# Delta rule: gate rows, two block turns and the inverse times the values on four 64x64 quarters of TensorE's array instead of two

## The chip, the cores and the metric

The kernel runs on one core of one Trainium2 chip. The metric is the device time of one execution in microseconds; the time before is the median of three runs.

## The reference

Two networks of two layers each run one after the other on 256 tokens of width 1024, in fp32. Each layer of the first has a feed-forward part, a mixer of three branches, and another feed-forward part. The branch that the change touches is a gated delta rule with 4 heads of width 128, computed in chunks of 64 tokens:

```python
decay = jnp.exp(jnp.where(causal, g_cum[..., :, None] - g_cum[..., None, :], -jnp.inf))
lower = jnp.where(strict, jnp.einsum('nbhid,nbhjd->nbhij', k_beta, k) * decay, 0.0)
rhs = jnp.concatenate([v * beta[..., None], k_beta * jnp.exp(g_cum)[..., None]], axis=-1)
uw = lax.linalg.triangular_solve(eye + lower, rhs, left_side=True, lower=True, unit_diagonal=True)
attn = jnp.einsum('nbhid,nbhjd->nbhij', q, k) * decay
...
v_new = u_c - jnp.einsum('bhcd,bhdv->bhcv', w_c, state)
o_c = jnp.einsum('bhcd,bhdv->bhcv', q_c, state) + jnp.einsum('bhij,bhjv->bhiv', a_c, v_new)
```

256 tokens make 4 chunks, and with 4 heads there are 16 blocks of 64x64. Outside the branch the mixer multiplies gates, `sigmoid(x @ w_gate + b_gate)`, with the branches' projections, and the second network has convolutions, pooling and sparse attention, which the change leaves alone.

## The kernel before, in words

**Weights.** Nearly all the time goes into products with weights that stream from HBM. Each weight tile of 128x1024 fp32 is split by ScalarE (`WH`, L989) and VectorE (`WL`, L1373) into a high and a low part, and TensorE makes three products of it (L467 to L469, L464 to L466, L560 and L561). Up to six split tiles are held, and ScalarE refills one when TensorE has ended with it.

**The delta rule.** `delta` (L3035 on) writes its own steps out by hand and calls `fill(n)` between them. A fill takes a step of the other branches' products with weights (`others`, L2997): gates, products of branch b, then of branch c. Each engine runs its instructions strictly in this written order, so what is queued behind a waiting instruction waits too.

**Blocks.** The 16 blocks lie in tiles of 128x512: chunk c of a pair of chunks on the partitions `HALVES[c]`, eight blocks side by side. The steps in order: sums of the gates (L644 on); `gd_rows` (L658), which spreads them into rows; `gd_decay` on VectorE (L1707), which subtracts the rows from the sums into `gDD` (L1711) and adds the mask (L1715); the products of keys and queries (L685) with their diagonals and square roots; `gd_lower` (L1736), which ends with `gLL` (L1744); `gd_attend` with `gQKD` (L1750); `gd_base` with `gBB` (L1760, L1763); `gd_flip` (L689), which turns the blocks of `gLL` and then of `gQKD` by a product with the identity (L695), and `gd_flipped` on ScalarE (L1131), which copies them to `gLT` and `gAT` (L1134); masks on GpSimd (L2189); five levels of the inverse (`level_first` L706, `level_mid` L1139 and L1141, `level_second` L718, L724, L726, `level_add` L1769 to L1777); `gd_apply` (L729): inverse times values, 128 columns wide (L737), and keys times inverse (L744); `gd_applied` (L1144) copies the results to `gUU` (L1148) and `gWT` (L1152); then the states.

**Quarters.** `HALVES` are the partitions 0 to 63 and 64 to 127. A 64x64 product reads its operands from one half of the partitions and writes PSUM on one half: the quarter of the array. `gd_rows`, `gd_flip` and the first part of `gd_apply` write to the half that they read from, so they use two quarters of the array, in turn. The levels already take all four: `QUADRANTS` (L95) adds the two crossed pairs. Crossed results come out on the other half of the partitions and in a second bank, and are moved back in two instructions of 64 partitions each (`CROSSED`).

**Banks.** PSUM has eight banks, handed out in a queue: `bank` takes the one at the front together with the event that empties it, and `drop` puts it at the end with the event that will.

```python
def bank(self):
    n, emptied = self.banks.pop(0)
def drop(self, b, *events):
    self.banks.append((b.n, list(events)))
```

TensorE waits for a bank's event (`emptied`, L459) before it writes. A branch's product, for instance, is emptied by `MG` (L1850), VectorE's product of gate and branch.

Of the kernel before, what the change touches and what calls it, by code (L numbers as in the profile page):

```python
# [8 lines left out]
ALU = mybir.AluOpType  # L9
# [5 lines left out]
P = 128  # L15
# [82 lines left out]
def csl(g):  # L98
    return slice(g * 64, g * 64 + 64)
# [356 lines left out]
class TensorProgram(Program):  # L456
# [198 lines left out]
            ins = self.e.matmul(k.PS[:, b.n, 16 + 8 * c:24 + 8 * c], chunk, gg, start=True, stop=True)  # L655
        ins.then_inc(*self.s["mm"].up(b.full))

    def gd_rows(self, l, b):  # L658
        k = self.k
        self.wait_ge("gdn_v", (l, "gg"))  # L660
        self.emptied(b)
        for g in range(8):
            for r in HALVES:
                ins = self.e.matmul(k.PS[r, b.n, csl(g)], k.sc["GG"][r, g:g + 1].to_broadcast([64, 64]), k.cm["tri"][r, r],
                                    start=True, stop=True)
        ins.then_inc(*self.s["mm"].up(b.full))

    def gd_turn(self, l, j0, t, b):
        k = self.k
# [16 lines left out]
                                    start=True, stop=True)  # L686
        ins.then_inc(*self.s["mm"].up(b.full))

    def gd_flip(self, l, n, b):  # L689
        k = self.k  # L690
        self.wait_ge("gdn_v", (l, n))
        self.emptied(b)
        for g in range(8):
            for r in HALVES:
                ins = self.e.matmul(k.PS[r, b.n, csl(g)], k.W[n][r, g, :], k.ident[r, r], start=True, stop=True)  # L695
        ins.then_inc(*self.s["mm"].up(b.full))

    def level_first(self, l, n, b, bx):
        k = self.k
# [29 lines left out]
    def gd_apply(self, l, ub, wb):  # L729
        k = self.k  # L730
        self.wait_ge("gdn_v", (l, "bt", 5))
        self.wait_ge("gdn_v", (l, "vbt", 1))
        for t in range(2):
            self.emptied(ub[t])
            for h in range(4):
                for r in HALVES:
                    ins = self.e.matmul(k.PS[r, ub[t].n, tsl(h)], k.W["BT"][r, 4 * t + h, :], k.W["VBT"][r, 4 * t + h, :],  # L737
                                        start=True, stop=True)
            ins.then_inc(*self.s["mm"].up(ub[t].full))
        for b in wb:  # L740
            self.emptied(b)
        for g in range(8):
            for c, r in enumerate(HALVES):
                ins = self.e.matmul(k.PS[:, wb[c].n, csl(g)], k.W["KBE"][r, g, :], k.W["BT"][r, g, :], start=True, stop=True)  # L744
        ins.then_inc(*self.s["mm"].up(wb[0].full, wb[1].full))
# [222 lines left out]
class ScalarProgram(Program):  # L968
# [154 lines left out]
        self.wait_ge("const_v", "eps")  # L1123
        self.e.activation(k.NR, k.NR, ACT.Sqrt, bias=k.eps[1e-6]).then_inc(*self.s["gdn_a"].up((l, "rs")))

    def gd_decay(self, l, b):
        k = self.k
        self.wait_ge("gdn_v", (l, "dm"))
        self.e.activation(k.W["DD"], k.W["DD"], ACT.Exp).then_inc(*self.s["gdn_a"].up((l, "dd")))

    def gd_flipped(self, l, n, to, b):  # L1131
        k = self.k
        self.wait_ge("mm", b.full)
        self.e.activation(k.WF[to], k.PS[:, b.n, :], ACT.Copy).then_inc(*self.s["gdn_a"].up((l, to)))  # L1134

    def level_mid(self, l, n, b, bx):
        k = self.k
# [5 lines left out]

    def gd_applied(self, l, ub, wb):  # L1144
        k = self.k
        for t in range(2):
            self.wait_ge("mm", ub[t].full)
            self.e.activation(k.W["UU"][:, 4 * t:4 * t + 4, :], k.PS[:, ub[t].n, :].rearrange("p (h n) -> p h n", h=4),  # L1148
                              ACT.Copy).then_inc(*self.s["gdn_a"].up((l, "uu", t)))
# [186 lines left out]
class VectorProgram(Program):  # L1336
# [367 lines left out]
        self.wait_ge("gdn_a", (l, "ex"))  # L1704
        self.e.tensor_tensor(tok["B3"], tok["B2"], k.EX[:, 0:8], ALU.mult).then_inc(*up((l, "b3")))

    def gd_decay(self, l, b):  # L1707
        k = self.k
        self.wait_ge("mm", b.full)
        self.wait_ge("gdn_v", (l, "gc"))  # L1710
        self.e.scalar_tensor_tensor(out=k.W["DD"], in0=k.PS[:, b.n, :].rearrange("p (g n) -> p g n", g=8), scalar=-1.0,  # L1711
                                    in1=over(k.sc["GC"], 64), op0=ALU.mult,
                                    op1=ALU.add).then_inc(*self.s["gdn_v"].up((l, "dr")))
        self.wait_ge("gdn_v", (l, "dr"))
        self.e.tensor_tensor(k.W["DD"], k.W["DD"], heads(k.half["decay"], 8),  # L1715
                             ALU.add).then_inc(*self.s["gdn_v"].up((l, "dm")))
# [673 lines left out]
class Walk:  # L2390
# [644 lines left out]
    def delta(self, l, fill, ot, free):  # L3035


        k, e = self.k, self.e
        b = self.bank()
        e.gate_sums(l, b)  # L3040
        e.gate_summed(l, b)
        self.drop(b, ("gdn_v", (l, "gc")), ("gdn_a", (l, "ex")))
        b = self.bank()
        e.gd_rows(l, b)
        e.gd_decay(l, b)
        self.drop(b, ("gdn_v", (l, "dr")))
        b1, b = self.bank(), self.bank()
        e.gd_products(l, 4, 4, b1)
        e.gd_diag(l, 4, "DS", b1)
        e.gd_products(l, 0, 0, b)  # L3050
        e.gd_diag(l, 0, "LL", b)
        self.drop(b, ("gdn_v", (l, "square", 0)))
        fill(2)
        e.gd_factors(l, free)
        b2, bk = self.bank(), [self.bank(), self.bank()]
        e.gd_products(l, 0, 4, b2)
        for t in range(2):
            e.gd_turn(l, 4, t, bk[t])
        fill(2)
        e.gd_lower(l, b1)  # L3060
        self.drop(b1, ("gdn_v", (l, "LL")))
        e.gd_attend(l, b2)
        self.drop(b2, ("gdn_v", (l, "QKD")))
        e.gd_base(l, "bb", "LL")
        fill(3)
        b1, b2 = self.bank(), self.bank()
        e.gd_flip(l, "LL", b1)
        e.gd_flipped(l, "LL", "LT", b1)
        self.drop(b1, ("gdn_a", (l, "LT")))
        e.gd_flip(l, "QKD", b2)  # L3070
        e.gd_flipped(l, "QKD", "AT", b2)
        self.drop(b2, ("gdn_a", (l, "AT")))
        e.gd_keys(l, 0, bk[0])
        self.drop(bk[0], ("gdn_v", (l, "kdc", 0)))
        e.gd_base(l, "bt", "LT")
        fill(2)
        e.gd_keys(l, 1, bk[1])
        self.drop(bk[1], ("gdn_v", (l, "kdc", 1)))
        for t in range(2):
            b = self.bank()  # L3080
            e.gd_turn(l, 8, t, b)
            e.gd_values(l, t, b)
            self.drop(b, ("gdn_v", (l, "vbt", t)))
        fill(2)
        for n, sz in enumerate((2, 4, 8, 16, 32)):
            e.level_mask(l, n, sz)
            b1, b2, last = self.bank(), self.bank(), sz == 32
            e.level_first(l, n, b1, b2)
            fill(2)
            e.level_mid(l, n, b1, b2)  # L3090
            for b in (b1, b2):
                self.drop(b, ("gdn_a", (l, "pw", n)))
            b1, b2 = self.bank(), self.bank()
            e.level_second(l, n, b1, b2, last)
            e.level_add(l, n, b1, b2, last)
            self.drop(b1, ("gdn_v", (l, "bt" if last else "bb", n + 1)))
            self.drop(b2, ("gdn_v", (l, "bt", n + 1)))
            fill(2)
        ub, wb = [self.bank(), self.bank()], [self.bank(), self.bank()]
        e.gd_apply(l, ub, wb)  # L3100
        e.gd_applied(l, ub, wb)
        for n in range(2):
            self.drop(ub[n], ("gdn_a", (l, "uu", n)))
        for n in range(2):
            self.drop(wb[n], ("gdn_a", (l, "wt", n)))
        fill(4)
        for t in range(2):
            bb = self.bank()
            ba = None
            for c in range(2):  # L3110
                if t or c:
                    b = self.bank()
                    ba = ba or self.bank()
                    e.gd_state(l, t, c, b, ba)
                    e.gd_new(l, t, c, b)
                    self.drop(b, ("gdn_v", (l, "vn", 2 * t + c)))
                    fill(2)
                if t and c == 0:
# [445 lines left out]
```

## Time and profile before

| | |
|---|---|
| median of 3 runs | 2267.87 us (2265.51 to 2268.32) |
| profiled execution | 2265.44 us, its span 2263.6 us |
| TensorE busy | 2232.2 us, 99% of the span |
| VectorE busy | 1631.1 us, 72% |
| ScalarE busy | 1198.2 us, 53% |
| GpSimd busy | 129.2 us, 6% |
| mean granted TensorE clock | 0.999 |
| HBM | 179 GB/s over the span |

The profiler's names: PE is TensorE, PEld its weight loads, DVE VectorE, ACT ScalarE, POOL GpSimd. Ends of matmuls are modelled, so starts are what to compare: from the start of one group to the start of the next. A chain of waits goes back from the last instruction, at each step to what released it or to what stood before it on its engine; a piece's length there is how much the end of the run moves past it.

### The profile page before, as it was taken

How to read it: one execution, taken by the hardware profiler on the slowest of the kernel's cores; microseconds unless marked ns; L12 is line 12 of the kernel's file. 1: busy time of each engine (PE TensorE's matmuls, PEld its weight loads, DVE VectorE, ACT ScalarE, POOL GpSimd, SP SyncE). 2: the span in 40 equal slices, each digit the busy share in tenths (PEclk: the TensorE clock that was granted, in tenths of full speed). 3: DMA queues.
4: the chain of work that ended last, by engine and by line, in shares of the span. 5: the costliest groups of instructions: out<-in, count | busy, mean ns of one | idle time of the engine just before them, and what ended most of it. 6: DMA issues, size and time to landing. Idle time of an engine off the chain costs nothing.

```text
span 2263.6 us, 34596 instructions
## 1 busy us (share of the span) xinstructions
PE 2232.2 (99%) x14127; PEld 1910.7 (84%) x14127; DVE 1631.1 (72%) x2503; ACT 1198.2 (53%) x1892; POOL 129.2 (6%) x185
## 2 busy tenths in 40 slices
PE   8999999999999999999999999999999999989999
PEld 7888899877888888888898777888878888867887
DVE  5777767867777776768668867776877778666776
ACT  5555446644555546554356544655454655556553
POOL 2100010120000000000100210000000000420000
PEclk9999999999999999999999999999999999999999
DMA  6755664445565556555564436655655656643654
GB/s 227 224 188 192 197 215 123 142 131 182 190 190 190 185 193 207 186 186 196 194 189 132 141 122 207 201 189 184 211 166 168 205 188 202 195 131 119 197 176 149
DMA packets 283567, 408.17 MB, mean 180 GB/s; under 512 B 13700, under 2 KB 170688, under 8 KB 283152
## 3 DMA queue, kind: packets, MB, share of 16 engines
q1 hardware_dynamic: 275600, 380.91, 52.4%
q0 software_dynamic: 7808, 25.04, 3.6%
q8 instruction: 112, 1.84, 0.3%
q14 instruction: 47, 0.39, 0.1%
HBM read 403.98 MB, written 1.91 MB: 179 GB/s over the span
## 4 chain that ended last, share of the span: by engine, by line
PE 88%; DVE 7%; ACT 3%; issue 1%; DMA 1%; POOL 0%; SPq 0%; DVEq 0%; ACTq 0%
PE PS L561 24%; PE PS L467 12%; PE PS L469 12%; PE PS L468 12%; PE PS L560 11%; PE PS L464 2%; PE PS L466 2%; PE PS L465 2%; DVE WL L1373 2%; PE PS L563 2%; PE PS L484 1%; PE PS L544 1%; PE PS L543 1%; PE PS L542 1%; DVE QX L1670 1%; ACT WH L989 1%
## 5 line engine op out<-in xcount | busy, mean ns | idle before, releaser
L1373 DVE TENSOR_TENSOR WL<-RW,WH 128x1024 fp32r<-128x1024 f32 x682 | 809.9, 1221 | 168.2 <-ACT WH L989 164.0
L561 PE MATMUL PS<-XT,WH 128*128 128x512 f32 x2368 | 807.9, 394 | 0.0
L989 ACT ACTIVATE WH<-RW 128x1024 fp32r<-128x1024 f32 x682 | 685.6, 1042 | 214.9 <-PE PS L469 46.8
L560 PE MATMUL PS<-XT,WL 128*128 128x256 f32 x2072 | 580.8, 280 | 0.0
L561 PEld LDWEIGHTS PS<-XT,WH 128*128 128x128 f32 x2368 | 425.1, 188 | 76.1
L560 PEld LDWEIGHTS PS<-XT,WL 128*128 128x128 f32 x2072 | 389.9, 188 | 13.4
L467 PE MATMUL PS<-WH,XT 128*128 128x512 f32 (+4 forms) x640 | 248.8, 389 | 4.6 <-DVE WL L1373 2.9
L469 PE MATMUL PS<-WH,XT 128*128 128x512 f32 (+4 forms) x640 | 240.0, 375 | 0.0
L468 PE MATMUL PS<-WL,XT 128*128 128x512 f32 (+4 forms) x640 | 239.5, 374 | 0.0
L467 PE MATMUL PS<-WH,HTH 128*128 128x512 f32 x488 | 192.4, 394 | 0.0
L469 PE MATMUL PS<-WH,HTL 128*128 128x512 f32 x488 | 191.7, 393 | 0.0
L468 PE MATMUL PS<-WL,HTH 128*128 128x512 f32 x488 | 191.5, 392 | 0.0
L464 PE MATMUL PS<-XT,WH 128*128 128x256 f32 x560 | 163.2, 291 | 1.6 <-DVE Z L1557 1.0
L1445 DVE TENSOR_TENSOR HM<-PS,HM 128x256 f32<-128x256 f32 x148 | 62.4, 422 | 133.1 <-ACT HM L1026 133.1
L465 PE MATMUL PS<-XT,WL 128*128 128x256 f32 x560 | 157.3, 281 | 0.0
L466 PE MATMUL PS<-XT,WH 128*128 128x256 f32 x560 | 157.2, 281 | 0.0
L467 PEld LDWEIGHTS PS<-WH,XT 128*128 128x128 f32 x640 | 120.8, 189 | 37.6 <-DVE XT L1384 8.9
L1026 ACT ACTIVATE HM<-PS 128x256 f32<-128x256 f32 x148 | 56.7, 383 | 169.8 <-PE PS L561 166.6
L469 PEld LDWEIGHTS PS<-WH,XT 128*128 128x128 f32 x640 | 120.9, 189 | 23.5
L468 PEld LDWEIGHTS PS<-WL,XT 128*128 128x128 f32 x640 | 121.1, 189 | 19.2
L1026 ACT ACTIVATE SG<-PS 128x256 f32<-128x256 f32 x148 | 54.1, 380 | 122.2 <-PE PS L561 120.9
L464 PEld LDWEIGHTS PS<-XT,WH 128*128 128x128 f32 x560 | 106.0, 189 | 6.1 <-issue 2.6
(504 smaller groups left out, 3219.5 us busy)
## 6 DMA issues: line engine op xcount, KB each, us to landing
RW<-in_w_ff_in SPq DMA_DIRECT2D x256, 512.0 KB, 4.4
RW<-in_w_ff_out SPq DMA_DIRECT2D x128, 512.0 KB, 4.5
RW<-in_w_in SPq DMA_DIRECT2D x56, 512.0 KB, 4.7
RW<-in_w_gate SPq DMA_DIRECT2D x48, 512.0 KB, 4.2
RW<-in_ffn_gate SPq DMA_DIRECT2D x44, 512.0 KB, 4.4
RW<-in_ffn_up SPq DMA_DIRECT2D x44, 512.0 KB, 4.3
RW<-in_ffn_down SPq DMA_DIRECT2D x44, 512.0 KB, 4.5
RW<-in_w_out SPq DMA_DIRECT2D x16, 512.0 KB, 4.8
```

The lines of the kernel that those rows point to most:

```text
L464: self.e.matmul(o, wh, xh, start=start, stop=False)
L465: self.e.matmul(o, wl, xh, start=False, stop=False)
L466: return self.e.matmul(o, wh, xl, start=False, stop=stop)
L467: self.e.matmul(o, xh, wh, start=start, stop=False)
L468: self.e.matmul(o, xh, wl, start=False, stop=False)
L469: return self.e.matmul(o, xl, wh, start=False, stop=stop)
L560: self.e.matmul(k.PS[:, b.n, 0:T], wl, k.XTH[:, kt, :], start=False, stop=False)
L561: ins = self.e.matmul(k.PS[:, b.n, :], wh, k.XT[:, kt, :], start=kt == 0, stop=kt == 7)
L989: self.e.activation(u.hi_out, raw, ACT.Copy).then_inc(*self.s["hi"].up(u.n))
L1026: self.e.activation(f[2 + part][:, n, j * T:j * T + T], self.k.PS[:, b.n, 0:T], ACT.Copy).then_inc(*self.s["ffn_a"].up((seq, sl, n, part, j)))
L1373: self.e.tensor_tensor(u.lo_out, raw, u.hi_out.bitcast(F), ALU.subtract).then_inc(*self.s["lo"].up(u.n))
L1445: self.e.tensor_tensor(v, self.k.PS[:, b.n, T:2 * T], v, ALU.add).then_inc(*self.s["ffn_v"].up((seq, sl, n, part, j)))
```

## The change

Three steps of the delta rule take all four quarters. `gd_rows` and both calls of `gd_flip` send half of their blocks (columns 256 to 511) through the crossed quarters into a second bank; `gd_apply` sends the values' second tile (`t = 1`) through the crossed quarters. The number of matmuls is the same. VectorE's subtraction and ScalarE's copies become three instructions each, one of 128x256 and two of 64x256. `gd_applied` copies the second half of `gUU` in two instructions of 64x512, and after `gWT` instead of ahead of it. `gd_rows` and each `gd_flip` take two banks instead of one, so the queue of banks stands otherwise from here on.

```diff
-    def gd_rows(self, l, b):
+    def gd_rows(self, l, b, bx):
...
         self.emptied(b)
-        for g in range(8):
-            for r in HALVES:
-                ins = self.e.matmul(k.PS[r, b.n, csl(g)], k.sc["GG"][r, g:g + 1].to_broadcast([64, 64]), k.cm["tri"][r, r],
-                                    start=True, stop=True)
-        ins.then_inc(*self.s["mm"].up(b.full))
+        self.emptied(bx)
+        for g, (r, to) in product(range(4), QUADRANTS):
+            g, bank = (g, b) if r is to else (g + 4, bx)
+            ins = self.e.matmul(k.PS[to, bank.n, csl(g)], k.sc["GG"][r, g:g + 1].to_broadcast([64, 64]), k.cm["tri"][r, r],
+                                start=True, stop=True)
+        ins.then_inc(*self.s["mm"].up(b.full, bx.full))
...
-    def gd_flip(self, l, n, b):
+    def gd_flip(self, l, n, b, bx):
         k = self.k
         self.wait_ge("gdn_v", (l, n))
         self.emptied(b)
+        self.emptied(bx)
+        for g, (r, to) in product(range(4), QUADRANTS):
+            g, bank = (g, b) if r is to else (g + 4, bx)
+            ins = self.e.matmul(k.PS[to, bank.n, csl(g)], k.W[n][r, g, :], k.ident[r, r], start=True, stop=True)
+        ins.then_inc(*self.s["mm"].up(b.full, bx.full))
...
-        for t in range(2):
-            self.emptied(ub[t])
-            for h in range(4):
-                for r in HALVES:
-                    ins = self.e.matmul(k.PS[r, ub[t].n, tsl(h)], k.W["BT"][r, 4 * t + h, :], k.W["VBT"][r, 4 * t + h, :],
-                                        start=True, stop=True)
-            ins.then_inc(*self.s["mm"].up(ub[t].full))
+        for b in ub:
+            self.emptied(b)
+        for h, (r, to) in product(range(4), QUADRANTS):
+            t = 0 if r is to else 1
+            ins = self.e.matmul(k.PS[to, ub[t].n, tsl(h)], k.W["BT"][r, 4 * t + h, :], k.W["VBT"][r, 4 * t + h, :],
+                                start=True, stop=True)
+        ins.then_inc(*self.s["mm"].up(ub[0].full, ub[1].full))
...
-        self.e.activation(k.WF[to], k.PS[:, b.n, :], ACT.Copy).then_inc(*self.s["gdn_a"].up((l, to)))
+        self.e.activation(k.WF[to][:, 0:256], k.PS[:, b.n, 0:256], ACT.Copy)
+        for r, rx in CROSSED:
+            ins = self.e.activation(k.WF[to][r, 256:512], k.PS[rx, bx.n, 256:512], ACT.Copy)
+        ins.then_inc(*self.s["gdn_a"].up((l, to)))
...
+        self.wait_ge("mm", ub[1].full)
+        for r, to in CROSSED:
+            ins = self.e.activation(k.W["UU"][r, 4:8, :], k.PS[to, ub[1].n, :].rearrange("p (h n) -> p h n", h=4), ACT.Copy)
+        ins.then_inc(*self.s["gdn_a"].up((l, "uu", 1)))
...
+        subtract(slice(0, P), slice(0, P), b, slice(0, 4))
+        for r, to in CROSSED:
+            ins = subtract(r, to, bx, slice(4, 8))
...
-        b1, b2 = self.bank(), self.bank()
-        e.gd_flip(l, "LL", b1)
-        e.gd_flipped(l, "LL", "LT", b1)
-        self.drop(b1, ("gdn_a", (l, "LT")))
-        e.gd_flip(l, "QKD", b2)
-        e.gd_flipped(l, "QKD", "AT", b2)
-        self.drop(b2, ("gdn_a", (l, "AT")))
+        for n, to in (("LL", "LT"), ("QKD", "AT")):
+            b1, b2 = self.bank(), self.bank()
+            e.gd_flip(l, n, b1, b2)
+            e.gd_flipped(l, n, to, b1, b2)
+            for b in (b1, b2):
+                self.drop(b, ("gdn_a", (l, to)))
```

On TensorE at the two turns of layer 0 the instructions and what they wait for stand as follows before. `gLL` and `gQKD` are what is turned, `WH` and `WL` the split weights of the next fill; `s_gdn_v` counts VectorE's steps of the delta rule, `s_gate_v` those on gates and branches, `s_lo` the weights' low parts.

```order
L695 MATMUL PS<-CO,gLL 64x64 [waits s_gdn_v]
L695 MATMUL PS<-CO,gLL 64x64 x15
L695 MATMUL PS<-CO,gQKD 64x64 [waits s_gdn_v]
L695 MATMUL PS<-CO,gQKD 64x64 x15
L467 MATMUL PS<-WH,XT 128x512 [waits s_lo]
```

And in the changed kernel (the function has moved from L695 to L697):

```order
L697 MATMUL PS<-CO,gLL 64x64 [waits s_gdn_v]
L697 MATMUL PS<-CO,gLL 64x64 x15
L697 MATMUL PS<-CO,gQKD 64x64 [waits s_gate_v]
L697 MATMUL PS<-CO,gQKD 64x64 x15
L467 MATMUL PS<-WH,XT 128x512 [waits s_lo]
```

The instructions stand where they stood; the turn of `gQKD` waits for the semaphore of the gates and branches instead of that of the delta rule.

On VectorE, from the subtraction on, before (`GT` are the gates of the two halves of the tokens, `MG` gate times branch, `SX` small tables, `CO` constants):

```order
L1711 SCALAR_TENSOR_TENSOR gDD<-PS,SX 128x512 [waits s_gdn_v,s_mm]
L1715 TENSOR_TENSOR gDD<-gDD,CO 128x512 [waits s_gdn_v]
...
L1744 TENSOR_TENSOR gLL<-PS,gDS 128x512 [waits s_gdn_v]
L1750 TENSOR_TENSOR gQKD<-PS,gDD 128x512 [waits s_mm]
L1760 SCALAR_TENSOR_TENSOR gBB<-gLL,CO 128x512 [waits s_gdn_v]
L1763 TENSOR_TENSOR gBB<-gBB,CO 128x512 [waits s_gdn_v]
L1850 TENSOR_TENSOR MG<-PS,GT_102 128x512 [waits s_gate_a,s_mm]
L1850 TENSOR_TENSOR MG<-PS,GT_103 128x512 [waits s_gate_a,s_mm]
```

And in the changed kernel:

```order
L1721 SCALAR_TENSOR_TENSOR gDD<-PS,SX 128x256 [waits s_gdn_v,s_mm]
L1721 SCALAR_TENSOR_TENSOR gDD<-PS,SX 64x256 x2
L1730 TENSOR_TENSOR gDD<-gDD,CO 128x512 [waits s_gdn_v]
...
L1759 TENSOR_TENSOR gLL<-PS,gDS 128x512 [waits s_gdn_v]
L1765 TENSOR_TENSOR gQKD<-PS,gDD 128x512 [waits s_mm]
L1775 SCALAR_TENSOR_TENSOR gBB<-gLL,CO 128x512 [waits s_gdn_v]
L1778 TENSOR_TENSOR gBB<-gBB,CO 128x512 [waits s_gdn_v]
L1865 TENSOR_TENSOR MG<-PS,GT_102 128x512 [waits s_gate_a,s_mm]
L1865 TENSOR_TENSOR MG<-PS,GT_103 128x512 [waits s_gate_a,s_mm]
```

Only the subtraction differs: three instructions for one. The two `MG` stand fourth and fifth behind `gLL` in both.

## Rows read from the trace of the kernel before

**Rows 1.** The page: busy time, and the chain that ended last by engine.

```profile
PE 2232.2 (99%) x14127; PEld 1910.7 (84%) x14127; DVE 1631.1 (72%) x2503; ACT 1198.2 (53%) x1892; POOL 129.2 (6%) x185
PE 88%; DVE 7%; ACT 3%; issue 1%; DMA 1%; POOL 0%; SPq 0%; DVEq 0%; ACTq 0%
```

**Rows 2.** Chain of waits, layer 0: start us, length us, what.

```profile
417.58 0.70 DVE gDD L1711
...
425.81 2.36 DVE WL L1373 x2
...
428.81 0.70 DVE gLL L1744
429.56 2.08 PE PS L695 x64
431.64 0.43 PE PS L467
...
438.28 0.62 PE PS L706 x32
...
477.50 1.89 PE PS L737 x32
479.39 1.93 PE PS L744 x32
```

**Rows 3.** Timeline of TensorE, layer 0: start, length, operation, idle before.

```profile
414.09 1.15 PE L664 MATMUL PS<-CO,SX 64*64 64x64 f32 x32
415.17 1.55 PE L685 MATMUL PS<-QX 128*64 128x64 f32 x45
...
429.56 1.15 PE L695 MATMUL PS<-CO,gLL 64*64 64x64 f32 x32 [0.31 <-DVE gLL L1744]
```

**Rows 4.** Who waited for whom, TensorE, whole run: total us, times, longest.

```profile
PE PS L724 <- ACT gPW L1141: 1.2, 2, 0.6
```

**Rows 5.** Timeline of VectorE, layer 0: at the subtraction, the turns, the last level.

```profile
418.31 0.78 DVE L1715 TENSOR_TENSOR gDD<-gDD,CO 128x512 f32<-128x512 f32 x1
...
429.42 0.68 DVE L1750 TENSOR_TENSOR gQKD<-PS,gDD 128x512 f32<-128x512 f32 x1
...
431.34 1.28 DVE L1850 TENSOR_TENSOR MG<-PS,GT 128x512 f32<-128x512 f32 x2
...
474.60 0.42 DVE L1774 SCALAR_TENSOR_TENSOR gBT<-PS,gBT 128x256 f32<-128x256 f32 x1 [0.42 <-PE PS L718]
475.93 1.29 DVE L1850 TENSOR_TENSOR GT<-PS,GT 128x512 f32<-128x512 f32 x2
```

**Rows 6.** Timeline of ScalarE, layer 0: a turn's copy, a level's copies, the apply's.

```profile
430.75 0.60 ACT L1134 ACTIVATE gLT<-PS 128x512 f32<-128x512 f32 x1 [1.74 <-PE PS L695]
...
438.98 0.38 ACT L1139 ACTIVATE gPW<-PS 128x256 f32<-128x256 f32 x1 [0.93 <-PE PS L706]
439.37 0.77 ACT L1141 ACTIVATE gPW<-PS 64x256 f32<-64x256 f32 x2
...
481.37 1.09 ACT L1152 ACTIVATE gWT<-PS 128x512 f32<-128x512 f32 x2 [1.33 <-PE PS L744]
484.39 1.06 ACT L989 ACTIVATE WH<-RW 128x1024 fp32r<-128x1024 f32 x1 [1.93 <-PE PS L469]
```

**Rows 7.** Chain of waits, layer 1, the two turns.

```profile
1256.84 2.08 PE PS L695 x64
```

**Rows 8.** Two near stalls of the second network: timeline of TensorE.

```profile
1998.57 0.66 PE L929 MATMUL PS<-CO,PA 128*128 128x128 f32 x4 [2.14 <-DVE PA L2084]
2001.47 1.12 PE L906 MATMUL PS<-CO,PCM 128*128 128x128 f32 x4 [2.25 <-DVE PCM L2051]
```

**Rows 9.** Busy times and granted clock by stretch, right after the second stall.

```profile
core 0: us, PE busy (x) PEld busy (x) DVE busy (x) ACT busy (x) POOL busy (x), PEclk, DMA share, GB/s
2001.50:2003.00 1.50, 1.50 (x7) 1.50 (x8) 1.50 (x2) 0.37 (x1) 0.00 (x0) 0.50 0.09 36
2003.00:2006.00 3.00, 3.00 (x20) 2.75 (x18) 2.25 (x4) 3.00 (x11) 2.38 (x4) 0.76 0.74 227
```

More of the change, by code:

```diff
@@ L692, in gd_flip @@
         self.emptied(b)
-        for g in range(8):
-            for r in HALVES:
-                ins = self.e.matmul(k.PS[r, b.n, csl(g)], k.W[n][r, g, :], k.ident[r, r], start=True, stop=True)
-        ins.then_inc(*self.s["mm"].up(b.full))
+        self.emptied(bx)
[3 more added lines that the diff above has]
+        ins.then_inc(*self.s["mm"].up(b.full, bx.full))
     def level_first(self, l, n, b, bx):
@@ L732, in gd_apply @@
         self.wait_ge("gdn_v", (l, "vbt", 1))
-        for t in range(2):
-            self.emptied(ub[t])
-            for h in range(4):
-                for r in HALVES:
-                    ins = self.e.matmul(k.PS[r, ub[t].n, tsl(h)], k.W["BT"][r, 4 * t + h, :], k.W["VBT"][r, 4 * t + h, :],
-                                        start=True, stop=True)
-            ins.then_inc(*self.s["mm"].up(ub[t].full))
+        for b in ub:
[5 more added lines that the diff above has]
+        ins.then_inc(*self.s["mm"].up(ub[0].full, ub[1].full))
         for b in wb:
@@ L1124, in gd_factors, with gd_decay @@
         self.e.activation(k.NR, k.NR, ACT.Sqrt, bias=k.eps[1e-6]).then_inc(*self.s["gdn_a"].up((l, "rs")))
-    def gd_decay(self, l, b):
+    def gd_decay(self, l, b, bx):
         k = self.k
@@ L1129, in gd_decay, with gd_flipped @@
         self.e.activation(k.W["DD"], k.W["DD"], ACT.Exp).then_inc(*self.s["gdn_a"].up((l, "dd")))
-    def gd_flipped(self, l, n, to, b):
+    def gd_flipped(self, l, n, to, b, bx):
         k = self.k
         self.wait_ge("mm", b.full)
-        self.e.activation(k.WF[to], k.PS[:, b.n, :], ACT.Copy).then_inc(*self.s["gdn_a"].up((l, to)))
+        self.e.activation(k.WF[to][:, 0:256], k.PS[:, b.n, 0:256], ACT.Copy)
+        for r, rx in CROSSED:
+            ins = self.e.activation(k.WF[to][r, 256:512], k.PS[rx, bx.n, 256:512], ACT.Copy)
+        ins.then_inc(*self.s["gdn_a"].up((l, to)))
     def level_mid(self, l, n, b, bx):
@@ L1145, in gd_applied @@
         k = self.k
[L1146 to L1149, printed above, removed]
+        self.wait_ge("mm", ub[0].full)
+        self.e.activation(k.W["UU"][:, 0:4, :], k.PS[:, ub[0].n, :].rearrange("p (h n) -> p h n", h=4),
+                          ACT.Copy).then_inc(*self.s["gdn_a"].up((l, "uu", 0)))
         for c in range(2):
@@ L1705, in gd_factors, with gd_decay @@
         self.e.tensor_tensor(tok["B3"], tok["B2"], k.EX[:, 0:8], ALU.mult).then_inc(*up((l, "b3")))
-    def gd_decay(self, l, b):
+    def gd_decay(self, l, b, bx):
         k = self.k
@@ L1710, in gd_decay, with subtract @@
         self.wait_ge("gdn_v", (l, "gc"))
-        self.e.scalar_tensor_tensor(out=k.W["DD"], in0=k.PS[:, b.n, :].rearrange("p (g n) -> p g n", g=8), scalar=-1.0,
-                                    in1=over(k.sc["GC"], 64), op0=ALU.mult,
-                                    op1=ALU.add).then_inc(*self.s["gdn_v"].up((l, "dr")))
+        def subtract(r, rows, bank, g):
+            return self.e.scalar_tensor_tensor(out=k.W["DD"][r, g, :],
+                                               in0=k.PS[rows, bank.n, :].rearrange("p (g n) -> p g n", g=8)[:, g, :], scalar=-1.0,
+                                               in1=over(k.sc["GC"][r, g], 64), op0=ALU.mult, op1=ALU.add)
+        subtract(slice(0, P), slice(0, P), b, slice(0, 4))
+        for r, to in CROSSED:
+            ins = subtract(r, to, bx, slice(4, 8))
+        ins.then_inc(*self.s["gdn_v"].up((l, "dr")))
         self.wait_ge("gdn_v", (l, "dr"))
@@ L3042, in delta @@
         self.drop(b, ("gdn_v", (l, "gc")), ("gdn_a", (l, "ex")))
[L3043 to L3046, printed above, removed]
+        b, bx = self.bank(), self.bank()
+        e.gd_rows(l, b, bx)
+        e.gd_decay(l, b, bx)
+        for b in (b, bx):
+            self.drop(b, ("gdn_v", (l, "dr")))
         b1, b = self.bank(), self.bank()
@@ L3101, in delta @@
         e.gd_applied(l, ub, wb)
-        for n in range(2):
-            self.drop(ub[n], ("gdn_a", (l, "uu", n)))
+        self.drop(ub[0], ("gdn_a", (l, "uu", 0)))
         for n in range(2):
             self.drop(wb[n], ("gdn_a", (l, "wt", n)))
+        self.drop(ub[1], ("gdn_a", (l, "uu", 1)))
         fill(4)
```

## Prediction

> **What bounds the kernel now.** I read the page first. TensorE is busy 99% of the span and the chain that ended last lies on it for 88% [rows 1]. So a TensorE second saved is a second gained only where TensorE is the last to arrive, and each new wait of TensorE costs its full length. A difference under 0.2% (4.5 us) is more than a measurement of this kernel can tell from none.
>
> Next comes the chain of waits through the delta rule of layer 0, which starts at 414 us, and of layer 1, 827.28 us later. It shows two regimes. From 404 to 429.5 us it runs on VectorE and ScalarE: the decay row `gDD`, a weight split `WL`, then `gLL` [rows 2]. TensorE waits for `gLL` at the first turn, if only 0.31 us [rows 3]. From 429.56 us on the chain is TensorE's, with an interruption of 0.57 us at two of the five levels; the list of waits gives one of those lines, 1.2 us over both layers [rows 4]. The reader is to see in the VectorE rows what follows `gLL`: `gQKD`, the two `gBB`, then the two `MG` products, which end at 431.34 + 1.28 = 432.62 us [rows 5].
>
> **Price of a quadrant.** One fp32 product of 64x64 stands as two records. On two diagonal quarters: both turns take 2.08 us for 64 records, 32.5 ns each; the inverse times values, 128 columns wide, 1.89 us for 32, 59 ns each. On all four: L706, the same 32 records as one turn, takes 0.62 us, 19.4 ns each [rows 2]. The same 32 for the gate rows run from 414.09 to 415.17, 1.08 us, which I take as a turn's 1.04 and a step to another shape [rows 3].
> - Gate rows: 1.04 to 0.62, saves 0.42 us of TensorE.
> - Each turn: 1.04 to 0.62, saves 0.42.
> - Inverse times values: no row has four quarters with 128 columns. Floor 0.62 us (128 columns can't be cheaper than 64), ceiling 1.89 (the same 32 records; L706 shows that alternating quarters adds nothing). The diagonal rows fit columns/2.4 GHz plus 5.8 ns (26.7 + 5.8 = 32.5, 53.3 + 5.7 = 59); four quarters halve the first term (13.3 + 6.1 = 19.4). So 26.7 + 6 = 32.7 ns, 1.05 us: saves 0.84. This is nearest to the L706 row, the same scheme on the same array.
>
> The L706 row shows 19.4 ns between records of 64 columns. The Trainium skill ("TensorE: Matmul & The Clock Gate", back-to-back issue gap) puts an isolated warm gap at columns/2.4 + 2.5 ns and never under 25 ns. By that rule 32 records of 128 columns would take 32 x 55.8 = 1.79 us and the apply would save 0.1 us, not 0.84; the measured row already lies below the rule's 29 ns, so I go by the row.
>
> **Price of the copies.** The crossed halves must be moved back, in three instructions for one. VectorE: one `gDD` of 512 columns runs from 417.58 to 418.31, 0.73 us; the same three shapes stand at the last level, 474.60 to 475.93, 1.33 us [rows 5]. So **+0.60 us on VectorE**. ScalarE: 0.38 + 0.77, less an overlap, about 1.1 us for each turn against 0.60 [rows 6]; what hides it comes below. For `gUU` one more 128x512 copy's time, about 0.55 us (the two `gWT` take 1.09).
>
> **Stage 1, gate rows.** The 0.60 us stands on the chain: `gDD` delays the reductions, the root on ScalarE, its table loads, the gates' additions, the `WH` copies, `WL`, `gLL`. I find no slack along it: each step is released by the step before. So `gLL` ends at 430.10 instead of 429.50, and `MG` at 433.22. TensorE's 0.42 us is lost: it arrives at 428.83 and waits.
>
> **Stage 2, the two turns: the step that decides.** Each now needs two banks at its start. Banks are handed out first in, first out, and at this place the queue in both layers is: the one that `gLL` empties, the one that `gQKD` empties, and the two that `MG` empties. Before, the turn of LL took the first, the turn of QKD the second, both of which each turn had to wait for anyway. Now the turn of LL takes the first two, and **the turn of QKD takes the two that MG empties**; the order of TensorE shows its wait move from the gdn to the gate semaphore. So:
> - LL waits for `gQKD`, which ends 0.60 us after `gLL`: starts at 430.75, ends 431.37.
> - QKD waits for the second `MG`: starts at 433.28, ends 433.90.
> Before, the weights' matmuls after the turns began at 431.64 [rows 2]. Behind the turns on TensorE's queue is everything. Shift: 433.90 - 431.64 = **+2.26 us**, with TensorE idle about 1.9 us twice. The bounds: +0.35 if `MG` were somehow done (431.99 - 431.64); +2.9 if VectorE loses another 0.6 us. Nothing later gives it back: what follows is TensorE's own chain, its two level waits are tied to its own results, and filler work can't be pulled ahead.
>
> **Cover of the rest.** The `gAT` copy ends near 435.0, and the first mask on GpSimd 1.3 us later, about 436.3; its level starts only at 438.28 + 2.26. That slack is over 4 us. ScalarE's longer `gUU` is put behind `gWT`: with the apply shorter by 0.84 all four end about 482.7 in the old time (482.46 - 0.84 + 1.1), and `WH` was idle 1.93 us before 484.39, waiting for TensorE [rows 6]. If that cover were gone, each layer would lose 0.55 us. The other waits for extra banks (gate rows, `gd_turn`) are for events several us old.
>
> **Sum.** Per layer +2.26 - 0.84 = +1.42; layer 1 has the same queue and the same chain (its turns also take 2.08 us [rows 7]). Two layers: **+2.84 us**, 0.13%. The profiled execution took 2265.44 us, so it becomes 2268.28. The median of the runs shown is 2.43 us above it, so on the median 2270.7.
>
> **Rivals.**
> - *The clock falls (slower side).* The chip showed what two near stalls do at 1998 us: idle 2.14, 0.66 of work, idle 2.25 [rows 8], and the granted clock then stood at 0.50 of full speed (1.2 instead of 2.4 GHz) through 1.5 us and, at a mean of 0.76, for half of the next 3 us [rows 9]. From 2001.47 that is some 2.9 us of work at half speed, 1.5 lost. Here: idle 1.9, 0.62 of work, idle 1.9, altogether 4.4 us against 5.05. For it: nearly the same pattern. Against: shorter by 0.6. The Trainium skill says in the clock gate section of the same page that activity releases the throttle and idleness brings it back; the trace agrees. Price 1.5 a layer: 2272.2 with one, 2273.7 with both. It decides if the three together come near those 5.05 us; with both the kernel is 0.26% slower.
> - *MG is not in the way.* Only the wait for `gQKD` stays: per layer +0.35 - 0.84 = -0.49; total -1.0, 2266.9. For it: little; `MG` stands behind `gQKD` and both `gBB` in VectorE's order.
> - *TensorE's saving counts in full.* Were VectorE hidden: 0.42 x 3 + 0.84 = 2.1 a layer, -4.2, 2263.7. Against: the wait at the first turn already exists.
> - *Four quarters do not help the wide product* (the change not doing what it says there): 2.26 - 0.0 a layer, +4.5, 2272.4. For it: no such row. Against: L706.
>
> **How the numbers follow.** Forecast 0.52; clock 0.24; MG not in the way 0.08; full saving 0.04; wide product unchanged 0.07; 0.05 for others. The likeliest is 2270.7. Its own range, with the apply between its bounds narrowed to 0.8 and 1.4 us, and the run's own spread of 2.8 us, is 2268.5 to 2272.7; the clock case reaches to 2273.7, MG's down to 2266.9. So 2267.0 to 2274.0. Slower by over 4.5 us: the clock case with more than one stall or a dear apply, 0.15, half of the unchanged product, 0.04, and tails, 0.05: 0.24. Faster by over 4.5: 0.03. Within: 0.73.
>
> **What would show it.** `gDD` in three pieces of 0.44 us; TensorE idle near 1.9 us before each turn, the second released by `MG`; 32 records in 0.62 us for each turn and 1.05 for the apply; +1.4 us between the first weights' matmul before the gate rows and that after the apply. It would be wrong if the turn of QKD follows that of LL at once, if the granted clock between 433 and 437 us is under 1, or if the apply stays at 1.89.

## The result, and the profile after

The changed kernel takes **2277.24 us**, the median of five runs (2276.38 to 2278.09), against 2267.26 us for the kernel before in its five. The ratio is 1.0041, with a 95% interval of 1.003 to 1.0052: slower by about 10 us. The forecast was 2270.7 and its range ended at 2274.0: the time lies above it. The profiled execution took 2276.38 us, its span 2274.6, so 11.0 us more than the one before.

The page of the changed kernel, busy times and the chain by engine:

```profile
PE 2233.9 (98%) x14127; PEld 1911.4 (84%) x14127; DVE 1631.4 (72%) x2507; ACT 1201.5 (53%) x1902; POOL 128.3 (6%) x185
PE 88%; DVE 7%; ACT 3%; DMA 1%; issue 1%; POOL 0%; SPq 0%; DVEq 0%; ACTq 0%
```

Against [rows 1] TensorE has the same number of instructions and even 1.7 us more of busy time, although three steps use the array twice as densely. So something else made matmuls longer. The list of who waited for whom, TensorE:

```profile
PE PS L697 <- DVE gQKD L1765: 5.4, 2, 2.7
...
PE PS L697 <- DVE MG L1865: 3.2, 2, 1.8
```

The two waits are the foretold ones: the first turn waits for `gQKD`, the second for `MG`. But the first is 2.7 us long in each layer, not 1.9. Timeline of TensorE, layer 0 and the same place of layer 1:

```profile
414.49 0.69 PE L665 MATMUL PS<-CO,SX 64*64 64x64 f32 x32
415.11 2.08 PE L686 MATMUL PS<-QX 128*64 128x64 f32 x64
...
431.90 1.13 PE L697 MATMUL PS<-CO,gLL 64*64 64x64 f32 x32 [2.71 <-DVE gQKD L1765]
434.42 1.13 PE L697 MATMUL PS<-CO,gQKD 64*64 64x64 f32 x32 [1.39 <-DVE MG L1865]
435.49 0.79 PE L467 MATMUL PS<-WH,XT 128*128 128x512 f32 x1
...
1262.85 0.69 PE L697 MATMUL PS<-CO,gLL 64*64 64x64 f32 x32 [2.70 <-DVE gQKD L1765]
1265.37 1.13 PE L697 MATMUL PS<-CO,gQKD 64*64 64x64 f32 x32 [1.83 <-DVE MG L1865]
```

The gate rows now go over to the next product after 0.62 us instead of 1.08 [rows 3]. The turns should show the same 0.69 us as the gate rows, and one does, at 1262.85. The other three show 1.13. Of the stretches at those places (busy time by engine, then PEclk, the granted clock):

```profile
core 0: us, PE busy (x) PEld busy (x) DVE busy (x) ACT busy (x) POOL busy (x), PEclk, DMA share, GB/s
430.00:432.00 2.00, 0.10 (x4) 0.13 (x8) 1.97 (x4) 0.28 (x1) 0.00 (x0) 0.79 0.89 292
432.00:434.00 2.00, 1.03 (x32) 0.84 (x32) 1.97 (x4) 0.89 (x3) 0.00 (x0) 0.50 0.59 214
434.00:436.00 2.00, 1.58 (x33) 1.47 (x34) 2.00 (x3) 0.64 (x2) 0.00 (x0) 0.50 0.04 12
436.00:438.00 2.00, 2.00 (x6) 1.53 (x5) 2.00 (x4) 0.76 (x2) 1.08 (x1) 0.50 0.70 183
438.00:440.00 2.00, 2.00 (x12) 1.66 (x12) 1.97 (x4) 0.25 (x1) 0.20 (x1) 1.00 0.71 218
1262.00:1264.00 2.00, 0.69 (x32) 0.59 (x32) 1.97 (x5) 0.39 (x2) 0.00 (x0) 1.00 0.97 349
1264.00:1266.00 2.00, 0.63 (x24) 0.66 (x28) 2.00 (x4) 0.75 (x2) 0.00 (x0) 0.50 0.14 53
```

The clock stood at half, 1.2 GHz, from about 431.2 to 438.0 us in layer 0 and from 1264.0 to 1270.9 in layer 1: 6.8 us each. In layer 0 it fell while TensorE was still idle ahead of the first turn. A wide product of weights (512 columns) follows the one before it after 0.43 us there (436.50 to 436.93) instead of 0.23 (438.35 to 438.58). Last, VectorE from the subtraction on:

```profile
417.99 1.29 DVE L1721 SCALAR_TENSOR_TENSOR gDD<-PS,SX 128x256 f32<-128x256 f32 x3
419.31 1.43 DVE L1730 TENSOR_TENSOR gDD<-gDD,CO 128x512 f32<-128x512 f32 x1
...
430.47 0.69 DVE L1759 TENSOR_TENSOR gLL<-PS,gDS 128x512 f32<-128x512 f32 x1
431.07 0.68 DVE L1765 TENSOR_TENSOR gQKD<-PS,gDD 128x512 f32<-128x512 f32 x1
...
433.00 1.28 DVE L1865 TENSOR_TENSOR MG<-PS,GT 128x512 f32<-128x512 f32 x2
```

The subtraction takes its three pieces in 1.3 us, as foreseen. The addition behind it takes 1.43 instead of 0.78 us [rows 5], and nobody had changed it.

### The profile page after: what moved, and what is told of

Its sections match the earlier page's. It is cut to its first block, busy times and chain, and to the rows that moved or that the text cites. A ratio compares the mean times of both kernels' runs of the same rounds, so it can differ in the third digit from the quotient of the medians.

```text
span 2274.6 us, 34614 instructions
## 1 busy us (share of the span) xinstructions
PE 2233.9 (98%) x14127; PEld 1911.4 (84%) x14127; DVE 1631.4 (72%) x2507; ACT 1201.5 (53%) x1902; POOL 128.3 (6%) x185
## 3 DMA queue, kind: packets, MB, share of 16 engines
q8 instruction: 112, 1.84, 0.3%
## 4 chain that ended last, share of the span: by engine, by line
PE 88%; DVE 7%; ACT 3%; DMA 1%; issue 1%; POOL 0%; SPq 0%; DVEq 0%; ACTq 0%
PE PS L561 24%; PE PS L467 12%; PE PS L469 12%; PE PS L468 12%; PE PS L560 11%; PE PS L464 2%; PE PS L466 2%; PE PS L465 2%; DVE WL L1381 2%; PE PS L563 2%; PE PS L484 1%; PE PS L544 1%; PE PS L543 1%; PE PS L542 1%; DVE QX L1678 1%
```

## Where the 11 us are

Starts of TensorE's groups, after minus before, give how late it is at each place:

| | layer 0 | layer 1 |
|---|---|---|
| gate rows | +0.40 | +4.08 |
| first turn | +2.34 | +6.01 |
| second turn | +3.88 | +7.55 |
| keys times inverse | +4.16 | +8.72 |

The delta stage, from the gate rows to keys times inverse, grew by 3.76 us in layer 0 and 4.64 in layer 1. The 0.40 ahead of it, and 2.3 us behind layer 1, lie outside of it; what the 2.3 us are is worked out further down.

The clock's part can be split off, because the second turn's start is set by VectorE. It starts 19.93 us behind the gate rows (434.42 - 414.49). With 0.62 us for the turn at full clock, the weights would follow at 20.55; before they followed at 17.48 (431.57 - 414.09). That is +3.07. The inverse times values took 1.03 instead of 1.89 us, -0.86. So **+2.21 us a layer without the clock**, and for the clock remain 1.55 and 2.43. That the second turn's start does not hang on the clock is seen in the run with a fill between the turns (below): in its layer 0 the clock held, and the turn starts 19.96 us behind the gate rows (434.05 - 414.09).

## The experiments

Each was compared with the kernel before on the same chip. The table gives ratio and interval, and the change of the delta stage's length (gate rows to keys times inverse) against 65.23 and 65.25 us, worked out from starts as above; "half" is the length of the spell at half clock near the turns. Both hold for the one profiled execution, while the time is the median of all: how often the clock falls differs between executions of one kernel. With a fill between the turns, for instance, the mean granted clock of the ten executions lies between 0.995 (the slowest, 2275.79 us) and 0.998 (the fastest, 2268.38, which is the profiled one).

| run | us | ratio | layer 0, layer 1 | half |
|---|---|---|---|---|
| after | 2277.24 | 1.0041 [1.003, 1.0052] | +3.76, +4.64 | 6.8, 6.8 |
| only inverse times values | 2266.82 | 0.9996 [0.9987, 1.0006] | -0.84, -0.87 | none |
| only gate rows | 2271.49 | 1.0018 [1.0009, 1.0027] | +1.25, +2.77 | none, 3.4 |
| only turns | 2274.62 | 1.003 [1.002, 1.0039] | +3.37, +3.34 | 3.4, 3.4 |
| GpSimd's product later | 2276.38 | 1.0038 [1.0024, 1.0053] | +3.66, +4.53 | 6.8, 6.8 |
| `gBB` later | 2274.56 | 1.0026 [1.0017, 1.0035] | +3.10, +2.41 | 6.8, 3.4 |
| a fill between the turns | 2270.75 | 1.0014 [1.0003, 1.0024] | +0.83, +1.96 | none, 3.4 |
| seven fills | 2292.36 | 1.0102 [1.0083, 1.0121] | +13.17, +13.09 | none |
| before, six fills | 2266.85 | 0.9996 [0.9987, 1.0005] | +0.93, +0.87 | none |
| whole change, six fills | 2264.22 | 0.9982 [0.9973, 0.9991] | -0.71, -0.71 | none |
| turns and values, six fills | 2263.45 | 0.9982 [0.9973, 0.9991] | -0.52, -0.54 | none |

### Each part alone

Inverse times values alone: the changed kernel with `gd_rows`, `gd_flip` and their readers as before.

```diff
-    def gd_rows(self, l, b, bx):
+    def gd_rows(self, l, b):
...
-    def gd_flip(self, l, n, b, bx):
+    def gd_flip(self, l, n, b):
```

> Only the inverse times the values on four quarters (its crossed copies behind gWT); gate rows and turns as before. All theories: 32 records in 1.03 us instead of 1.89 in each layer, nothing waits for the later copies, so 2 x 0.86 = 1.7 us less than before (ratio 0.9992), granted clock as before. If the crossed copies are in the way of the next WH: 1.7 - 1.1 = 0.6 us less.

Its chain of waits, layer 0:

```profile
478.24 1.03 PE PS L737 x32
479.28 1.93 PE PS L744 x32
```

1.03 us for what took 1.89 [rows 2]: 32.2 ns a record. The stage is shorter by 0.84 and 0.87 us, so this step keeps all that it saves. Two layers make 1.7 us, less than the comparison can tell from nothing: 0.9996.

Gate rows alone:

```diff
-    def gd_flip(self, l, n, b, bx):
+    def gd_flip(self, l, n, b):
...
-        for h, (r, to) in product(range(4), QUADRANTS):
+            for h in range(4):
+                for r in HALVES:
```

> Only the gate rows on four quarters, with VectorE's subtraction in three pieces; turns and apply as before. Theory A (VectorE's chain decides when the first turn can start): gLL ends 0.60 us later for the three pieces and 0.65 us more because the addition L1730 waits for GpSimd's product Z, so TensorE idles 0.31 + 0.42 + 1.25 = 2.0 us before the first turn and the kernel is 2 x 1.25 = 2.5 us slower; the clock stays at 1.00, since one idle stretch stands alone. Rival B (the loss is all in the turns' banks and the clock): 2 x 0.42 = 0.8 us faster.

Timelines of VectorE and of TensorE at both first turns, and the two stretches:

```profile
419.06 1.45 DVE L1723 TENSOR_TENSOR gDD<-gDD,CO 128x512 f32<-128x512 f32 x1
```

```profile
430.98 1.15 PE L696 MATMUL PS<-CO,gLL 64*64 64x64 f32 x32 [2.04 <-DVE gLL L1752]
...
1259.50 1.38 PE L696 MATMUL PS<-CO,gLL 64*64 64x64 f32 x32 [2.02 <-DVE gLL L1752]
```

```profile
430.00:432.00 2.00, 1.02 (x34) 1.02 (x36) 1.97 (x4) 0.04 (x1) 0.00 (x0) 1.00 0.92 314
1260.00:1262.00 2.00, 2.00 (x49) 2.00 (x46) 1.97 (x5) 0.60 (x1) 0.00 (x0) 0.56 0.71 254
```

It is 3.5 us slower, not the 2.5 expected, since the clock did not hold in layer 1. It is the best witness of two things. The addition is slow here too, so the gate rows' three-piece subtraction brings that, not the turns. And both layers have the same single idle stretch of 2.0 us, with the clock at 1.00 in one and fallen in the other: +1.25 against +2.77. So **one such stretch can be enough**, need not be, and costs 1.5 us when it is.

Turns alone:

```diff
-    def gd_rows(self, l, b, bx):
+    def gd_rows(self, l, b):
...
-        for h, (r, to) in product(range(4), QUADRANTS):
+            for h in range(4):
+                for r in HALVES:
```

> Only the two turns on four quarters, with their two banks each; VectorE's subtraction in one piece. Theory A (banks): LL waits for gQKD (idle 0.9 us), QKD for the second MG (idle 1.9 us); the matmuls after the turns start 1.66 us later in each layer, 3.3 us in all if the clock holds. If two near idle stretches of 0.9 and 1.9 us are enough to bring the clock down, another 1.5 to 2 us per layer, 6.5 to 7 us in all. Rival (the turns' waits follow only from VectorE's later subtraction): 2 x 0.84 = 1.7 us faster.

```profile
430.68 0.69 PE L696 MATMUL PS<-CO,gLL 64*64 64x64 f32 x32 [1.01 <-DVE gQKD L1754]
433.21 0.69 PE L696 MATMUL PS<-CO,gQKD 64*64 64x64 f32 x32 [1.83 <-DVE MG L1854]
```

With VectorE as it was, the queue of banks alone makes both waits, and the turns' 0.62 us is no use: +3.4 a layer, of which +1.84 without the clock (18.70 + 0.62 - 17.48, as above) and 1.5 for a spell of 3.4 us. In layer 0 both turns ran at full clock and it fell behind them; in layer 1 it fell within the second. The kernel is 6.6 us slower, as was expected for the case that the clock falls. In seven of the nine executions the mean granted clock was lower (0.995 to 0.997) than in the profiled one (0.998), so most of them had more low clock than is seen here.

### The addition and GpSimd's product

Before, GpSimd's product of `Z` and `SM` ran from 416.82 to 420.25 us, two instructions of 1.7 us each. The addition was issued at 418.31, 0.2 us before the first of them ended, and took 0.78. Now the subtraction ends later, the addition is issued at 419.31, inside the second of the two (418.92 to 420.20), and ends at 420.7; this second one takes 1.28 us. GpSimd's two timelines, before and after:

```profile
416.82 3.43 POOL L2173 TENSOR_TENSOR Z<-Z,SM 128x512 f32<-128x512 f32 x2 [24.06 <-ACT Z L1093]
```

```profile
417.22 2.98 POOL L2188 TENSOR_TENSOR Z<-Z,SM 128x512 f32<-128x512 f32 x2 [24.05 <-ACT Z L1095]
```

One of the two engines pays: GpSimd before (3.43 against 2.98 us), VectorE after (+0.65). The test moves GpSimd's product behind `gBS`:

```diff
     def z_gate(self, l, t):
+        return
+
+    def z_late(self, l, t):
...
                              ALU.mult).then_inc(*self.s["gdn_g"].up((l, "bs")))
+        for t in range(2):
+            self.z_late(l, t)
```

> The whole change, but GpSimd's product Z is issued behind its product BS, so it isn't running when VectorE adds the mask to gDD. Theory: L1730 takes 0.69 instead of 1.43 us, gLL ends 0.65 us earlier, and the idle before the first turn falls from 2.7 to 2.05 us. If the clock still falls in both layers: 1.3 us less than the changed kernel, 8.6 over before. If the shorter idle stretch lets the clock stay at 1.00: about 2.8 us over before, as predicted before the result. Rival (the addition is slow for its own reasons, the crossed write before it): L1730 stays at 1.43 and nothing changes.

```profile
419.23 0.69 DVE L1730 TENSOR_TENSOR gDD<-gDD,CO 128x512 f32<-128x512 f32 x1
...
426.64 2.80 DVE L1381 TENSOR_TENSOR WL<-RW,WH 128x1024 fp32r<-128x1024 f32 x2 [1.65 <-ACT WH L991]
```

```profile
424.69 2.54 POOL L2191 TENSOR_TENSOR Z<-Z,SM 128x512 f32<-128x512 f32 x2
```

The addition is back at 0.69 us although the subtraction ahead of it is still in three pieces, which confirms the collision and rules out the crossed pieces as its cause. But the product now reaches 427.23, and `WL`, issued at 426.64, takes 2.80 instead of 2.36: 0.44 of the gain is lost. The wait ahead of the first turn went from 2.7 to 2.4 us and the clock fell as before. Total: 8.4 us over before, near the 8.6 expected for this case, and no difference to the changed kernel (10.0 over) that can be told, since the intervals overlap. The Trainium skill ("SBUF — State Buffer", "Who interferes with whom") says that VectorE and GpSimd share a pair of ports, which is an exclusive lock, that a VectorE instruction with two inputs in SBUF contends with a GpSimd instruction that reads SBUF, and that the order of issue decides who blocks. These three runs agree with it: the addition takes 1.43 us when it is issued inside GpSimd's instruction and 0.69 with none near.

### The wait for MG

`gBB` issued behind the three fills, so that `MG` comes 1.3 us earlier:

```diff
-        e.gd_base(l, "bb", "LL")
         fill(3)
+        e.gd_base(l, "bb", "LL")
```

> The whole change, but the two gBB steps of VectorE are issued behind the fill, so both MG end 1.3 us earlier. Theory (the second idle stretch is the wait for MG's banks): the idle before the turn of QKD falls from 1.8 to about 0.5 us; the first, 2.7 us, stays. If the first alone brings the clock down as well: 2 x 1.3 = 2.6 us less than the changed kernel, 7.4 over before. If the clock holds with only one long stretch: another 3 us less, about 4 over before. Rival (the second wait has another cause, for instance that ScalarE's copies of LL must come first): no change.

The second wait fell from 1.8 us to 0.5 in one layer and went in the other, and the first stayed at 2.7. The clock still fell in both layers: in layer 0 ahead of the first turn, with no second wait behind it, in layer 1 right behind the second turn. The time is 7.1 us over before, against 7.4 expected for this case.

Then work for TensorE between the turns, one fill taken from the two that come later:

```diff
                 self.drop(b, ("gdn_a", (l, to)))
+            if n == "LL":
+                fill(1)
...
-        fill(2)
+        fill(1)
```

> The whole change, with one step of the fill (6 products with weights, 1.4 us) taken from behind the turns and put between them. Theory: the second idle stretch of 1.8 us holds 1.4 us of work, the first of 2.7 us stays: 2.8 us less than the changed kernel if the clock still falls in both layers, 7.2 over before; about 4 over before if it holds. Rival (idle stretches aren't the cost, the half clock from other causes is): no change.

Timeline of TensorE, and the stretches at the turns of layer 0 and 1:

```profile
431.52 0.69 PE L697 MATMUL PS<-CO,gLL 64*64 64x64 f32 x32 [2.73 <-DVE gQKD L1765]
...
434.05 0.69 PE L697 MATMUL PS<-CO,gQKD 64*64 64x64 f32 x32 [0.23 <-DVE MG L1865]
```

```profile
430.00:432.00 2.00, 0.48 (x32) 0.51 (x32) 1.94 (x4) 0.00 (x0) 0.00 (x0) 1.00 0.92 333
1260.00:1262.00 2.00, 2.00 (x27) 1.59 (x18) 1.97 (x5) 1.15 (x3) 0.00 (x0) 0.50 0.48 177
```

With the same 2.7 us of idleness the clock held in layer 0 and fell in layer 1. Their difference, 1.96 - 0.83 = 1.1 us, is again a price of a spell. Layer 0 also bears out the sum without the clock: +2.21 less a fill's 1.4 us is the +0.83 measured. The whole went from 10 us over before to about 3.

### Covering both waits

Both turns covered, two fills more ahead and seven in all instead of five:

```diff
-        fill(3)
+        fill(5)
...
+            if n == "LL":
+                fill(1)
...
-        fill(2)
+        fill(1)
```

> The whole change, with five steps of the fill ahead of the turns instead of three, one between them, and one behind instead of two. Theory: both waits are covered by work (2.8 us against 2.7, 1.4 us against 1.8), the clock stays at 1.00, and TensorE's savings of 0.42 + 0.84 + 0.86 us per layer count: 4.2 us less than before, ratio 0.998. The masks of GpSimd then come later against the first level by some 3 us, of a slack of over 4. Rival 1: that slack is used up and the first level waits, no faster than before. Rival 2: the changed kernel's loss isn't idle time and clock, so it stays at 8 to 10 us over before.

A miss, by far. Who waited for whom, TensorE:

```profile
PE PS L726 <- ACT gPW L1146: 18.7, 8, 4.7
```

The waits at the turns were gone (0.5 us in all), but the levels of the inverse waited up to 4.7 us for ScalarE's copies. The two fills more put the later ones out of step with the levels. ScalarE then had `WH`, which waits for TensorE to release a weight tile, ahead of the copy `gPW`, for which TensorE waited. The two longest of these waits in each layer, 4.7 and 3.0 us, were each followed by 3.4 us at half clock:

```profile
454.50 1.06 ACT L991 ACTIVATE WH<-RW 128x1024 fp32r<-128x1024 f32 x1 [5.79 <-PE PS L469]
456.72 1.06 ACT L991 ACTIVATE WH<-RW 128x1024 fp32r<-128x1024 f32 x1 [1.16 <-PE PS L469]
457.68 0.37 ACT L1144 ACTIVATE gPW<-PS 128x256 f32<-128x256 f32 x1
```

A control was needed: do the fills alone, with six in all, change the kernel before?

```diff
-        fill(3)
+        fill(5)
...
-        fill(2)
+        fill(1)
```

> The kernel before, with five steps of the fill ahead of the turns instead of three and one behind instead of two; no four-quarter step. It tells what the place of the fills alone is worth. Theory: only the idle of 0.31 us before the first turn goes, 0.6 us less than before, within the noise. Rival: the place of the fills alone gives what x7_fills_ahead gains, 4 us.

They do not: 0.9996, with 1.00 of the clock at both turns. The stage is 0.9 us longer since it holds one fill more, which is missing elsewhere. With the same six fills in the changed kernel, five ahead, one between and none behind:

```diff
-        fill(3)
+        fill(5)
...
+            if n == "LL":
+                fill(1)
...
-        fill(2)
```

> The whole change with five steps of the fill ahead of the turns, one between them and none directly behind: six in place of five up to here (x7_fills_ahead had seven, and its levels then stood behind a WH copy that waits for TensorE; x8_before_ahead had six and they did not). Theory: no wait over 0.3 us at the turns, clock at 1.00 there, no wait over 0.6 us in the levels; TensorE saves 0.31 + 0.42 + 0.84 + 0.86 = 2.4 us per layer: 4.5 us less than before, ratio 0.998. Rival 1: with no fill behind the turns the mask of GpSimd comes too late and the first level waits 1 to 3 us in each layer, no gain. Rival 2: ScalarE's copies of the levels wait again as in x7_fills_ahead, 20 us over before.

```profile
432.48 0.69 PE L697 MATMUL PS<-CO,gLL 64*64 64x64 f32 x32
...
435.00 0.69 PE L697 MATMUL PS<-CO,gQKD 64*64 64x64 f32 x32 [0.24 <-DVE MG L1865]
```

2264.22 us against 2268.16 on the same chip, 0.9982 [0.9973, 0.9991]: **this version beats both kernels**, the one before by 3.9 us, where 4.5 less were expected. That is less than the 4.5 us which the forecast took for the least that can be told, but with 11 and 21 executions the interval lies below 1. All parts of the change are in it. The stage is 1.6 us shorter in each layer than the control's (-0.71 - 0.93 and -0.71 - 0.87): a layer's foreseen 2.1 us less the 0.24 of wait, but for 0.3 us.

Last, the same without the gate rows (their three pieces on VectorE dropped too), with four fills ahead, one between and one behind:

```diff
-    def gd_rows(self, l, b, bx):
+    def gd_rows(self, l, b):
...
-        fill(3)
+        fill(4)
...
+            if n == "LL":
+                fill(1)
...
-        fill(2)
+        fill(1)
```

> Turns and apply on four quarters, gate rows as before, with four steps of the fill ahead of the turns, one between them, one behind (six in all). Theory: VectorE's chain is as before, gQKD ends 0.9 us after TensorE's old arrival and one more step of 1.4 us covers it; the clock holds; savings 0.31 + 0.84 + 0.86 = 2.0 us per layer: 4.0 us less than before, ratio 0.9982, and 0.5 us more than x9_cover_all at equal cover. Rivals as for x9_cover_all.

```profile
430.15 0.69 PE L696 MATMUL PS<-CO,gLL 64*64 64x64 f32 x32
...
432.36 0.69 PE L696 MATMUL PS<-CO,gQKD 64*64 64x64 f32 x32
```

2263.45 us, 0.9982 again. The gate rows on four quarters add nothing that can be told, even where their delay is covered; the two runs differ in the place of one fill too, so the rows' share alone was not measured.

## Why the prediction was wrong, step by step

- *Price of a quadrant: right.* The turns and gate rows at full clock take 0.62 us. The inverse times values was put at 1.05 us from the difference of rows and took 1.03. Going by the Trainium skill's gap ("TensorE: Matmul & The Clock Gate", back-to-back issue gap) it would have been 1.79: the runs decide for the row.
- *The bank queue: right.* Both waits and their releasers came as written, in the changed kernel and with the turns alone. `MG` was in the way. With `gBB` later, `MG` came 1.3 us earlier, and the second wait shrank from 1.8 to 0.5 us or went.
- *"So +0.60 us on VectorE" and "so gLL ends at 430.10": the first term that was mis-sized.* `gLL` came 1.65 us later than before in absolute time, 1.25 after the 0.40 that the gate rows were late already. The missing 0.65 is the addition's wait for GpSimd. I followed what released each step of VectorE, and did not look at what ran on GpSimd at the place to which the step was moved. It stands in the trace of before: a product of 3.43 us at 416.82. With it the second turn starts at 434.02 in the old time instead of 433.28, and the sum per layer is +2.21 instead of +1.42: 1.6 us in both. By itself this term leaves the time at 2272.3, inside the range.
- *The clock, put at nothing in the sum: the step that failed most, and the one that takes the time out of the range.* It was a rival at 0.24, since "it decides if the three together come near those 5.05 us". The runs showed neither condition nor chance to be right: a single idle stretch of 2.0 us was enough once out of two times, one of 2.7 in two cases out of three (a fill between the turns; `gBB` later, layer 0), and all six stages with two uncovered waits (the changed kernel, the turns alone, GpSimd's product later) fell. In layer 0 of the changed kernel it was down at 431.2 us, within the first wait, so the second had no part in that fall. [Rows 8, 9] show a case where it fell; I took what was large there for what is needed. The same trace has a case where it held, behind an idle stretch of 2.9 us (shown below), and one trace of each could not tell that it is a matter of chance. The rival's own price, 1.5 us a layer, fits one spell (1.1 to 1.5 measured) but not the changed kernel's double ones, 1.55 and 2.43. Together 4.0 us.
- *Cover of the rest: right in effect.* The level after the turns waited for nothing new. The `gUU` copy in two pieces took 1.20 us and was paid by ScalarE's slack.
- *The rest.* 2 x 1.42 = 2.84 foreseen, 1.6 from GpSimd's collision and small steps, 4.0 from the clock: 8.4 of the 11.0 us between the two profiled executions. Of the others, 0.40 lies ahead of layer 0's stage and 2.3 behind layer 1's. In that stretch both kernels wait 2.9 us for `HN` at the same place of the program. Timeline of TensorE and the stretch behind it, before and then after:

```profile
1674.62 0.63 PE L484 MATMUL PS<-CO,HN 128*128 128x128 f32 x4 [2.89 <-DVE HN L1438]
1674.00:1678.00 4.00, 3.36 (x16) 2.56 (x17) 1.82 (x3) 0.60 (x1) 1.58 (x6) 1.00 0.69 208
```

```profile
1683.27 0.52 PE L484 MATMUL PS<-CO,HN 128*128 128x128 f32 x3 [2.89 <-DVE HN L1446]
1683.00:1687.00 4.00, 3.73 (x12) 3.04 (x13) 1.48 (x3) 0.60 (x1) 1.57 (x6) 0.61 0.78 231
```

  The clock held in the kernel before and fell in the changed one, for 3.4 us. This is no effect of the change: in the twelve profiles of this case it fell at this place in nine, in that of the kernel before with other fills (x8_before_ahead) too, and held in three. The lateness is 8.65 us ahead of it and 9.91 behind it (1776.83 - 1766.92), so 1.3 of the 2.3 us are the kernel before having escaped the spell in its profiled execution, which at 2265.44 us is as fast as the fastest of its five. The spell behind the two near stalls of [rows 8, 9] is in both kernels, 10.2 us later in the changed one. A longer wait for a transfer (`Z`, 1.4 against 0.4 us) comes next, and the lateness grows by another 0.7 there; why it is longer was not tested. That accounts for the 11.0 us to about 0.3. Between the medians, which are 10.0 us apart, no such account can be made.

## What to carry to other kernels

A step on four quarters of the array takes a second bank here, and in a queue of banks that makes it wait for a reader that has nothing to do with it: look up who empties the bank that it will now get, and put work there before making the step shorter. Put a fall of the clock behind a new idle stretch into the sum, by its chance and price, and not beside it as a rival: here a single stretch of 2.0 to 2.9 us ended in one in 12 of 17 cases (1 of 2 at 2.0, 2 of 3 at 2.7, 9 of 12 at 2.9), and the two uncovered waits of a layer in all six. One profile can't give that chance, as the clock differs between executions. Where VectorE's work is moved by half a microsecond, look at GpSimd's row at the new place.

## What the hardware showed that was not expected

- The clock fell after a single idle stretch of 2.0 us in one layer and held through one of 2.7 us in another, at the same place of the program; at another place it fell behind 2.9 us in nine of twelve profiles and held in three. It then stood at half for 3.4 us or for 6.8.
- Its price is smaller than its length: 1.1 to 1.5 us for 3.4 us at half, 1.55 and 2.43 for 6.8, where TensorE was idle for 2.1 and 1.4 us of it (layer 0: 431.2 to 431.9 and 433.0 to 434.4; layer 1: 1264.0 to 1265.4).
- One instruction of 512 columns on VectorE took 1.43 instead of 0.69 us beside a product on GpSimd, and when that was moved, two others took 2.80 instead of 2.36.
- 64x64 records on four quarters follow each other after 19.4 ns with 64 columns and 32.2 ns with 128; on two quarters after 32.5 and 59.
